# Two more cache sequences laid out in 32-row blocks by transfers on chip, and turned in place by VectorE

## The reference, cut to what matters

```python
lat_past = cache_kv_latent[l, page_table].reshape(bs, past_len, MLA_KV_LORA)
kr_past = cache_k_rope[l, page_table].reshape(bs, past_len, MLA_ROPE)
q_lat = jnp.einsum('bqhd,chd->bqhc', q_nope, w_uk)
s_past = jnp.einsum('bqhc,bkc->bhqk', q_lat, lat_past) + jnp.einsum('bqhr,bkr->bhqk', q_rope, kr_past)
...
p = jax.nn.softmax(s, axis=-1)
ctx = jnp.einsum('bhqk,bkc->bqhc', p[..., :past], lat_past) + ...
```

## Time and profile before

| | |
|---|---|
| median of 3 runs | 1266.18 us (1266.0 to 1266.7) |
| the profiled execution's own time | 1266.02 us |
| its span, first to last instruction | 1264.2 us |
| granted TensorE clock | 0.998 of full speed |
| PE busy | 1250.9 us (99%) |
| DVE busy | 549.7 us (43%) |
| ACT busy | 250.5 us (20%) |
| DMA, mean | 157 GB/s |

### The profile page before, as it was taken

One profiled execution on the slowest core, in us unless ns is written; L12 is line 12 of the kernel. 1 busy time (PEld: TensorE's weight loads), 2 busy tenths in 40 slices (PEclk: granted clock), 3 DMA queues, 4 the chain that ended last, 5 costly groups with the idle time before them and its releaser, 6 DMA issues.

```text
span 1264.2 us, 18049 instructions
## 1 busy us (share of the span) xinstructions
PE 1250.9 (99%) x7142; PEld 1022.8 (81%) x7142; DVE 549.7 (43%) x1387; ACT 250.5 (20%) x640; POOL 153.0 (12%) x210
## 2 busy tenths in 40 slices
PE   8999999999999999999999999999999999999997
PEld 6878777776888888888888787777778888888886
DVE  7866646323235333321178746463241453324212
ACT  3432414311100111110033324243111011111000
POOL 2012442010000000020001134511000000000000
PEclk9999999999999999999999999999999999999999
DMA  9433576357454444464454344755564544444440
GB/s 342 155 100 101 134 254 227 130 188 170 122 152 148 147 143 147 148 225 150 148 154 142 100 115 150 249 205 177 140 173 126 149 143 149 150 150 150 151 138 35
DMA packets 93971, 198.49 MB, mean 157 GB/s; under 512 B 41680, under 2 KB 42736, under 8 KB 91072
## 3 DMA queue, kind: packets, MB, share of 16 engines
q1 hardware_dynamic: 84624, 156.15, 40.4%
q0 software_dynamic: 8768, 40.84, 9.4%
q10 hardware_dynamic: 496, 0.36, 0.1%
HBM read 183.86 MB, written 9.25 MB: 153 GB/s over the span
## 4 chain that ended last, share of the span: by engine, by line
PE 95%; DVE 4%; ACT 1%; issue 0%; DMA 0%; SPq 0%; DVEq 0%; ACTq 0%
PE banks L573 77%; PE banks L1063 2%; PE banks L1076 1%; PE banks L1111 1%; PE banks L1074 1%; PE banks L968 1%; PE banks L717 1%; DVE arena L1715 1%; PE banks L996 1%; PE banks L675 0%; PE banks L1012 0%; DMA arena<-in_x 0%; DVE arena L2114 0%; PE banks L873 0%; PE banks L590 0%
## 5 line engine op out<-in xcount | busy, mean ns | idle before, releaser
L573 PE MATMUL banks<-arena 128*128 128x264 f32 x4512 | 1032.3, 388 | 5.7 <-DVE arena L1609 4.9
L573 PEld LDWEIGHTS banks<-arena 128*128 128x128 f32 x4512 | 851.0, 190 | 169.2 <-issue 13.2
L1217 ACT ACTIVATE arena<-banks 128x256 f32<-128x256 f32 (+8 forms) x252 | 92.6, 391 | 403.7 <-PE banks L573 293.2
L2217 DVE TENSOR_SCALAR arena<-arena 128x256 f32<-128x256 f32 x44 | 18.2, 414 | 130.2 <-ACT arena L1217 130.0
L2250 DVE SCALAR_TENSOR_TENSOR arena<-banks,arena 128x264 f32<-128x264 f32 x16 | 6.9, 433 | 134.2 <-PE banks L573 134.2
L2431 POOL COPY arena<-arena 128x2 f32<-128x2 f32 x44 | 13.7, 310 | 377.6 <-ACT arena L1217 275.9
L1248 ACT ACTIVATE arena<-banks 128x264 f32<-128x264 f32 x32 | 12.6, 392 | 130.6 <-PE banks L573 130.6
L2110 DVE COPY arena<-banks 128x512 f32<-128x512 f32 x24 | 16.6, 690 | 36.7 <-PE banks L1063 36.5
L1529 ACT ACTIVATE arena<-arena 128x256 f32<-128x256 f32 x44 | 18.4, 417 | 66.3 <-DVE arena L2219 66.3
L2224 DVE SCALAR_TENSOR_TENSOR arena<-arena 128x256 f32<-128x256 f32 x44 | 18.7, 426 | 26.6 <-ACT arena L1529 26.6
L2229 DVE TENSOR_TENSOR arena<-arena,banks 128x256 f32<-128x256 f32 x42 | 17.7, 422 | 26.4 <-PE banks L573 26.3
(11 more groups left out here) (447 smaller groups left out, 1072.5 us busy)
## 6 DMA issues: line engine op xcount, KB each, us to landing
arena<-in_weights SPq DMA_DIRECT2D x229, 512.0 KB, 3.6
arena<-in_weights SPq DMA_DIRECT2D x113, 256.0 KB, 3.5
arena<-in_s POOLq DMA_DIRECT2D x2, 2048.0 KB, 10.9
out_ss_o<-arena POOLq DMA_DIRECT2D x16, 256.0 KB, 3.1
arena<-in_mla_w POOLq DMA_DIRECT2D x4, 1024.0 KB, 6.7
arena<-arena SPq DMA_DIRECT2D x64, 64.0 KB, 2.4
arena<-in_c POOLq DMA_DIRECT2D x4, 512.0 KB, 6.3
out_sc_o<-arena POOLq DMA_DIRECT2D x16, 128.0 KB, 3.8
```

Source lines behind the costliest of these rows:

```text
L573: mm = nc.tensor.matmul(dst, ring[:, at_:at_ + 128], rhs[:, j, :], start=(start and j == 0), stop=(stop and j == k - 1))
L1217: return A(dst, src, ACT.Copy, scale=scale)
L2217: link(ts(cv, fc[:, j % 3, 0:TP], w[0], par[:, Q_FB + j:Q_FB + j + 1], ALU.mult, ALU.add))
```

## The change

Sequences 4 and 5 take the way of 6 and 7, and the early work is redistributed:

- `IN_BLOCKS = 4, 5, 6, 7`. TensorE's 16 transposes a sequence, and the two copies each by ACT and DVE, are gone for 4 and 5.
- The blocks of 4 are laid in `ltt[:, 0]` and those of 5 in `ltt[:, 1]`, since no other place is free, and VectorE turns them in place there. SP waits for the scores of 2 before it issues the 16 transfers of 4 (`page_scored` 3), and for the scores of 3 (`ss` 0) before those of 5. Those of 6 and 7 wait for `cx` 0 as before.
- The places in SP's order come from `mark`: ahead of the weights of unit 53 (blocks of 4), 54 (5), 56 (6) and 57 (7). The formula is the one that gave 56 before, taken ahead of `pages(3)` and behind it for the new ones.
- DVE turns the key and the latents of 4 between `total(0)` and `newest(0)`, and those of 5 behind `combined(0)` and one half.
- Between pages 5 and pages 6 stand seven halves in place of four; the three are taken from the end of the list, behind `combine` 1.
- The bank of the second group's scores is opened at `cmb` 0 in the count of the banks.

The diff, cut to its core:

```diff
--- before.py
+++ after.py
@@ -21,6 +21,7 @@
 
 
 P = 128
+IN_BLOCKS = 4, 5, 6, 7
 D, KT = 1024, 8
 L = 2
 TP, NB = 256, 8
@@ -97,7 +98,15 @@
 
 def schedule():
 
-    s, piece = [], [0]
+    s, piece, marks = [], [0], {}
+
+    def mark(*sequences):
+        at_ = (34 + piece[0]) // 2 + SLOTS - 1
+        for n in sequences:
+            while at_ in marks:
+                at_ += 1
+            marks[at_] = n
+
 
     def add(name, n=1, reader="A", first=0):
         s.extend((name, i, reader) for i in range(first, first + n))
@@ -141,16 +150,19 @@
     add("sn", 1, "V"); add("ckB", 1, "V")
 
     def pages(n):
-        if n < 6:
+        if n not in IN_BLOCKS:
             s.extend(("ltr", 4 * n + i, "AV"[i % 2]) for i in range(4))
         half(1)
 
     for n in range(4):
+        if n == 3:
+            mark(4)
         pages(n)
+    mark(5)
     add("ss"); half(1); add("mxT", 1, "V"); half(1); add("mxB", 1, "V"); half(3); add("lsum", 1, "V"); add("cx")
-    at_context = (34 + piece[0]) // 2
+    mark(6, 7)
     half(2); add("cmb", 1, "V")
-    pages(4); half(2); pages(5); half(4); pages(6); pages(7); add("ss", 1, "A", 1)
+    pages(4); half(2); pages(5); half(7); pages(6); pages(7); add("ss", 1, "A", 1)
     half(2); add("mxT", 1, "V", 1); half(1); add("mxB", 1, "V", 1); half(4); add("lsum", 1, "V", 1); add("cx", 1, "A", 1); half(3); add("cmb", 1, "V", 1); half(len(PIECES) - piece[0])
     add("ov")
     add("wb", 8, "V"); add("pw", 8, "V")
@@ -158,7 +170,7 @@
     for j in range(1, FFC):
         s += [("fg", j, "A"), ("fu", j, "V")]
     add("fd", 8, "V")
-    return s, at_context + SLOTS - 1
+    return s, marks
 
 
 SCHED, BLOCKS_AT = schedule()
@@ -171,7 +183,7 @@
 def turn_banks():
 
 
-    first_page = {("ltr", 0): ("ss", 0), ("ltr", 16): ("ss", 1)}
+    first_page = {("ltr", 0): ("ss", 0), ("cmb", 0): ("ss", 1)}
     early = {e[0] for e in EARLY}
     bank_of, before, user, turn, held, mixed = {}, {}, {}, {8: -1, 6: -1, 2: -1}, set(), False
     for name, i, _ in SCHED:
@@ -199,7 +211,7 @@
 SIGNALS = dict(
     branch_c=8, c_decayed=1, c_loaded=32, conv=12, conv_state=1, conv_tanh=12, decay_exp=1,
     decay_masked=1, diag_set=3, ffn_conv=22, ffn_sconv=2, ffn_stanh=2, ffn_tail=22, ffn_tanh=22, ffn_zeros=1, fh_loaded=16,
-    hidden=2, hidden_norm=16, norm_raw=16, norm_square=16, norm_sum=14, hist_loaded=16, key_copied=2, key_turned=8, lat_turned=8, **{f"lat_blocks{n}": 256 for n in (6, 7)}, **{f"lat_in{n}": 32 for n in range(8)},
+    hidden=2, hidden_norm=16, norm_raw=16, norm_square=16, norm_sum=14, hist_loaded=16, key_copied=2, key_turned=8, lat_turned=16, **{f"lat_blocks{n}": 256 for n in IN_BLOCKS}, **{f"lat_in{n}": 32 for n in range(8)},
     inverse=1, inverse_turned=1, m_loaded=64, mdecay_exp=1, mdecay_in=4, mdecay_masked=1, merged=8, mla_q=16, mla_kv=16,
     msample_kv=1, mv_diag=1, n_loaded=32, neg_max=2, new_products=1, next_rows=1, 
     oa_scaled=1, oa_squares=1, oc_raw=1, oc_root=1, oc_inverse=1, oc_squares=1, ones_column=1, pads_zero=2,
@@ -457,9 +469,12 @@
         roots, totals = cols[:, 0:3], bank("fd", 0)[:, 0:3]
         last_rms = bank("fd", 1)[:, 0:TT]
 
+        def blocks(n):
+            return lat[n - 6] if n >= 6 else ltt[:, n % 2].rearrange("p i n -> p (i n)")
+
         def quarter_of_latents(n, b, q):
 
-            return (lat[n - 6][32 * q:32 * q + 32, 512 * b:512 * b + 512].rearrange("i (r j) -> i r j", r=NR),
+            return (blocks(n)[32 * q:32 * q + 32, 512 * b:512 * b + 512].rearrange("i (r j) -> i r j", r=NR),
                     lat[n][32 * b:32 * b + 32, :].rearrange("i (r q j) -> i r q j", r=NR, q=4)[:, :, q, :])
 
         def slot(j):
@@ -497,7 +512,14 @@
                 sp.dma_start(x[:, 2 * i:2 * i + 2, :].rearrange("p k n -> p (k n)"), a["x"][:, 2 * TT * i:2 * TT * (i + 1)]).then_inc(x_in[i], 16)
 
             def blocks_of_latents(l, n):
-                sp.wait_ge(*out(l, "cx", 0))
+                if n == 0:
+                    sp.wait_ge(*out(l, "uq", 7))
+                elif n == 4:
+                    sp.wait_ge(*at(l, "page_scored", 3))
+                elif n == 5:
+                    sp.wait_ge(*out(l, "ss", 0))
+                else:
+                    sp.wait_ge(*out(l, "cx", 0))
                 sp.wait_ge(*at(l, f"lat_in{n}", 32))
                 for b in range(4):
                     for q in range(4):
@@ -510,8 +532,8 @@
                         load_x(i)
                 if u >= SLOTS:
                     sp.wait_ge(w_started, u - SLOTS + 2)
-                if u % UNITS in (BLOCKS_AT, BLOCKS_AT + 1):
-                    blocks_of_latents(u // UNITS, 6 + u % UNITS - BLOCKS_AT)
+                if u % UNITS in BLOCKS_AT:
+                    blocks_of_latents(u // UNITS, BLOCKS_AT[u % UNITS])
                 for h, at_, n in runs[u]:
                     if u == 0 and at_ == 0:
                         for i in range(2):
@@ -1063,14 +1085,14 @@
                                 mm = nc.tensor.transpose(b[:, q * P:(q + 1) * P], lat[n][:, r_ * P:(r_ + 1) * P], ident)
                             mm.then_inc(out_ready, 1)
                     half(1)
-                    if n < 6:
+                    if n not in IN_BLOCKS:
                         pe.wait_ge(*evac(l, "ltr", 4 * n + 2))
                         pe.wait_ge(*evac(l, "ltr", 4 * n + 3))
                         pe.wait_ge(*at(l, "key_turned", n + 1))
                     else:
-                        pe.wait_ge(*at(l, "lat_turned", 4 * (n - 5)))
+                        pe.wait_ge(*at(l, "lat_turned", 4 * (IN_BLOCKS.index(n) + 1)))
                     for i in range(4):
-                        turned = heads(ltt[:, n % 2, i, :], 32) if n >= 6 else turned_lat(n)[:, :, 32 * i:32 * i + 32]
+                        turned = heads(ltt[:, n % 2, i, :], 32) if n in IN_BLOCKS else turned_lat(n)[:, :, 32 * i:32 * i + 32]
                         nc.tensor.matmul(heads(sb[32 * i:32 * i + 32, :], 32), ql_pad[:, g, s_, :], turned,
                                          start=(s_ == 0), stop=False, skip_group_check=True)
                     mm = nc.tensor.matmul(sb, qr_pad[:, g, s_, :], krt[:, n % 2, :], start=False, stop=(s_ == 3), skip_group_check=True)
@@ -1135,7 +1157,7 @@
                 pages(4)
                 half(2)
                 pages(5)
-                half(4)
+                half(7)
                 pages(6)
                 pages(7)
                 half(2)
@@ -1469,7 +1491,7 @@
                 act.wait_ge(*at(l, "st_conv", 16))
 
                 def pages(n):
-                    for i in (0, 2):
+                    for i in () if n in IN_BLOCKS else (0, 2):
                         act.wait_ge(*out(l, "ltr", 4 * n + i))
                         if n >= 2 and i == 0:
                             act.wait_ge(*scored(n - 2))
@@ -1501,7 +1523,7 @@
                 pages(4)
                 half(2)
                 pages(5)
-                half(6)
+                half(9)
                 half(3)
                 powers(1)
                 half(4)
@@ -2049,6 +2071,21 @@
                                              q_sum[:, :, 4 * g:4 * g + 4].rearrange("p h s -> p s h"))
                 last.then_inc(*up("query_blocks"))
 
+                def scored(n):
+
+                    if n % 4 == 3:
+                        return out(l, "ss", n // 4)
+                    return at(l, "page_scored", 3 * (n // 4) + n % 4 + 1)
+
+                def turn(n):
+                    dve.wait_ge(*at(l, f"lat_in{n}", 32))
+                    if n >= 2:
+                        dve.wait_ge(*scored(n - 2))
+                    V.transpose(krt[:, n % 2, :], key[n]).then_inc(*up("key_turned"))
+                    dve.wait_ge(*at(l, f"lat_blocks{n}", 256))
+                    for i in range(4):
+                        V.transpose(ltt[:, n % 2, i, :], blocks(n)[:, 512 * i:512 * i + 512]).then_inc(*up("lat_turned"))
+
                 def masked(g):
                     for h in range(4 * g, 4 * g + 4):
                         dve.wait_ge(*out(l, "sc", h))
@@ -2093,25 +2130,14 @@
                 dve.wait_ge(*at(l, "st_sn", 32))
                 dve.wait_ge(*at(l, "st_conv", 16))
 
-                def scored(n):
-
-                    if n % 4 == 3:
-                        return out(l, "ss", n // 4)
-                    return at(l, "page_scored", 3 * (n // 4) + n % 4 + 1)
-
                 def pages(n):
                     dve.wait_ge(*at(l, f"lat_in{n}", 32))
                     if n >= 2:
                         dve.wait_ge(*scored(n - 2))
                     V.transpose(krt[:, n % 2, :], key[n]).then_inc(*up("key_turned"))
-                    if n < 6:
-                        for i in (1, 3):
-                            dve.wait_ge(*out(l, "ltr", 4 * n + i))
-                            V.tensor_copy(ltt[:, n % 2, i, :], bank("ltr", 4 * n + i)).then_inc(*read("ltr", 4 * n + i))
-                    else:
```

(21 more changed lines are left out.)

## The result

The changed kernel takes 1276.32 us (median of 6 runs, 1274.54 to 1277.88) against 1266.21 us: a ratio of 1.0079, with a 95% interval of 1.0070 to 1.0089. It is slower by 10.1 us, where 4 us less were forecast, and lies outside the range.

The account below looks back on a forecast made before the run. TensorE, busy 99% of the span, was taken as the bound. Per layer, 3.60 us saved less 1.5 wait and 0.1 contention gave 2.0, 4.0 in all: 1262.2 us median, range 1258.6 to 1267.0.

Parts of the forecast that it names:

- TensorE's share: TensorE's list: transposes of 4 and 5 gone, 3.56 us, scores on contiguous views 0.04 us, together 3.60 us a layer.
- SP's queue as what decides: Four batches in SP's one queue: last transfer of 7 issued at 309.5, scores of 7 waiting 1.5 us more than before.
- the three signs of being wrong: Batch of 4 over 12.5 us, any weight waited for, or scores of 7 waiting no longer than 0.15 us.
- Together 11.5 us of work in 11.4 us: full, but just ... I take 0.1 us: DMA engines, 259.9 to 271.3: gathers' 5.6 us plus the batch of 4's 5.9 us just fit, slip 0.1 us.
- the mean: SP's time for one batch of 16 transfers, 11.27 us, from four earlier batches of 10.84 to 11.55 us.
- 1.8 (1.7 and the slip of 0.1): Before the scores of 7: TensorE waits 1.7 us for VectorE's turn, plus 0.1 us slip from DMA contention.
- The ring covers these: Queued weights 53 to 57 come in time; unit 56 issued at 297.6, needed at 307; 57 tight, some 2 us.
- the 2.4 to 4.0 that I had lent unit 57: Landing time in us borrowed from on-chip transfers for weights 57, issued at 310.3, there at 313 to 315, needed at 316.
- The rival "slower": Gathers hold back the blocks of 4, which slip 4.7 us with the queue behind: 1271.6 us, chance 0.14.
- Its point of decision: Slip of the batch of 4 from which the slower outcome decides: 3.3 us.
- a slip of 0.6 us: Batch of 4 beside the gathers: keeping half of each engine, 0.50 for 0.54 wanted, it loses 0.6 us, not 4.7.

Follow-up runs that it names:

- e11: Changed kernel with GpSimd issuing all four batches, newest row before turn of 4, SP three units less ahead on weights 54 to 60, ten halves: 1259.00 us, 0.9944.
- e1: Changed kernel with SP also waiting for the gather of sequence 7 before issuing the batch of 4: 1289.7 us in a single run.
- e5: Changed kernel with GpSimd issuing all four batches, SP issuing weights alone: 1272.38 us, ratio 1.0049.
- e9: Changed kernel with GpSimd issuing all batches, newest row before turn of 4, SP three units less ahead on weights 54 to 60, seven halves: 1270.07 us, 1.0037.
- e12: Changed kernel with GpSimd issuing all batches, newest row before turn of 4, weights as far ahead as before, ten halves: 1272.70 us, 1.0048.
- e4: Changed kernel with GpSimd issuing the batch of 7, SP keeping 4, 5 and 6: 1279.8 us, ratio 1.0109.
- e10: Changed kernel with GpSimd issuing all batches, newest row before turn of 4, weights as far ahead as before, seven halves: 1272.69 us, 1.0051.

## Why the prediction was wrong

- **TensorE's share, 3.60 us a layer: right.** 7.2 us in all; the run without the transfers gave 7.4, e11 7.3.
- **SP's queue as what decides, the order and the place of the wait: right.** The first start was off by 0.06 us, the long wait stands before the scores of 7. But the batches began at 259.99, 276.26, 290.19 and 303.80, where 260.1, 272.6, 286.2 and 298.7 were forecast; and two of the three signs of being wrong came: the batch of 4 took over 12.5 us, and weights were waited for. The 1.66 us before the scores of 5 in the second layer weren't forecast either.
- **"Together 11.5 us of work in 11.4 us: full, but just ... I take 0.1 us": this step failed.** The batch of 4 slipped by 3.7 and 5.1 us against 11.27. The path was right, but this term of the sum was mis-sized. I had added up engine time as if a packet cost the same in company as alone:

```profile
259.99:275.00 15.01, 15.01 (x79) 11.43 (x77) 3.62 (x9) 3.33 (x8) 1.91 (x2) 1.00 0.99 216
```

  That is 14.9 us of all sixteen for what I had put at 11.5, with about the same bytes. In the second layer it is 0.86 of 16.35, 14.1 us: the batch took longer there while the engines weren't full, so a better sum of engine time alone wouldn't give the slip. With the batch moved away it took 12.99 and 12.27 us, so 2.0 and 4.1 us of it are the gathers' company; the other 1.0 to 1.7 us are single slow transfers, which I had in the mean with one a batch at most. The other three came to 34.9 and 35.5 us, 1.1 and 1.7 above three times the mean. So the last batch ended at 314.61 and not 310.2, its blocks were turned 4.5 us later, TensorE itself was only 0.8 us late, and the wait became 5.45 us where 1.8 (1.7 and the slip of 0.1) was forecast.
- **"The ring covers these": wrong for unit 56.** It was issued at 302.60, not 297.6, and landed after 307, its due time: 0.6 to 0.7 us a layer. Its two transfers took 3.0 and 4.3 us to land, and those behind the last batch (issued from 314.66) 3.8 to 5.4, not the 2.4 to 4.0 that I had lent unit 57.
- **The clock was missing from the sum.** A wait of over 5 us costs more than itself: 3.0 and 1.8 us behind it at half clock.
- **The rival "slower"** had the right mechanism, gathers holding back the blocks of 4, if not its size (4.7 us from the gathers, where e1 gives 2.0 and 4.1), and its 1271.6 us came nearest; I gave it 0.14 because of the sum above. Its point of decision was set at 3.3 us and the slips were 3.7 and 5.1.
- The rule of the Trainium skill, DMA: Bandwidth & Descriptors, section Queues, rings and completion order (each engine takes turns between the queues), by which I had worked out a slip of 0.6 us, doesn't give the size: the gathers' company alone cost 2.0 and 4.1 us. That figure rests on e1 alone, one profile with two layers.

## What to carry to other kernels

Before adding transfers to a queue that also feeds the bound engine, write its timeline to the end: start, batches, and what stands behind them; if its end lies at the due time, a stretch goes nearly one to one into the bound engine. Adding less may be the better change: one batch more gained 4 us here, two more lost 10. Then look whether the engines behind the queue have room, and don't trust a sum of busy times where small packets meet other traffic (11.5 us of it became 14.9 and 14.1 here), since a second queue only helps if they do. If they don't, loads that nobody needs yet can be held back and covering work be moved ahead of the due time; here only both together paid.

## What was not expected of the hardware

- GpSimd issues these transfers as fast as SP does: 0.65 us each (10.37 us for 16) against 0.67.
- Two batches of 128-byte packets side by side, one from SP and one from GpSimd, stretch SP's to 19.60 us, where those of 5, 6 and 7 by themselves took 10.8 to 12.4; GpSimd's issue is hardly held up (64 transfers in 41.1 to 43.6 us in e5 and e9 to e12), but its landings are late (4.7 us after the issue in the median in e4, 7.7 in e5).
- After waits of 3.40 us (e9), 4.16 (e12), 5.45 and 7.07 us TensorE's next eight matmuls took 1.75 to 1.94 us where 1.06 is usual, at a granted clock of 0.50 to 0.57. A wait of 2.74 us (e10, second layer) was followed by 1.67 us at 0.60. But one of 3.42 us (four halves, first layer) left the group behind it at 1.06 and the clock at 1.00, so the length of the wait alone doesn't tell.
